# Reordering the first block of a two-block transformer kernel, and sharing the weight split between two engines

## The reference

```python
def first_block(x, c, ...):
    mod = silu(c) @ w_ada + b_ada                 # 2048 -> 6*2048
    shift_m, scale_m, gate_m, shift_f, scale_f, gate_f = split(mod, 6)
    h = rms_norm(x, norm_mix_g) * (1 + scale_m) + shift_m
    q, k, v, xs, z, bmat, cmat, dt_raw = split(h @ w_in)   # 1024 each up to z, 256, 256, 16
    attn = rms_norm(moba_attention(q, k, v, rel_bias), attn_norm_g)    # 8 heads
    ssm = ssd_mixer(xs, z, bmat, cmat, dt_raw, ...)        # 16 heads, conv of 4 taps first
    x = x + gate_m * (concatenate([attn, ssm]) @ w_out)
    h = rms_norm(x, norm_ffn_g) * (1 + scale_f) + shift_f
    x = x + gate_f * conv_ffn(h, w_up, ..., w_down)        # 2048 -> 2*5632 -> 2048
    return rms_norm(x, final_norm_g)

def second_block(x, mem, ...):
    # neighbourhood attention and latent attention side by side, w_out
    x = x + memory_attention(rmsnorm(x), rmsnorm(mem), w_xq, w_xk, w_xv, w_xo)
    x = x + swiglu(rmsnorm(x), w_gate, w_up, w_down)
    return rmsnorm(x, final_norm)
```

## Time and profile before

| | |
|---|---|
| median of 3 runs | 3294.6 us (3288.72 to 3298.83) |
| the profiled execution: span from first to last instruction | 3309.4 us |
| its own time beside the span | no separate time is listed; the span stands for it |
| busy: PE, POOL, ACT, DVE | 88%, 67%, 35%, 34% |
| granted clock of TensorE, mean (1.00 is 2.4 GHz) | 0.930 |

### The profile page before, as it was taken

How to read it: one execution, slowest core, us unless ns; L and a number is a source line. 1 busy time by engine, 2 the same in 40 slices (tenths; PEclk the granted TensorE clock), 3 DMA queues, 4 the chain that set the end, 5 groups by cost and what they waited for, 6 DMA issues and landing times.

```text
span 3309.4 us, 54043 instructions
## 1 busy us (share of the span) xinstructions
PE 2912.6 (88%) x21608; PEld 2795.5 (84%) x21608; DVE 1128.3 (34%) x1286; ACT 1167.9 (35%) x1286; POOL 2220.5 (67%) x889
## 2 busy tenths in 40 slices
PE   4657879896789999999997976698898999999997
PEld 4657769775779999999997975598798999999997
DVE  4688771256855444422213032302102000001222
ACT  2222223332233433334443443233333333333443
POOL 2455768353758889878884843085476888887885
PEclk8778999798999999999998987698999999999999
DMA  7976765432746666545552542053243554554452
GB/s 218 351 267 241 272 250 207 166 142 81 261 176 226 229 219 238 191 164 179 187 180 90 189 129 90 8 221 129 102 164 129 180 187 179 181 187 165 178 184 96
DMA packets 112195, 598.17 MB, mean 181 GB/s; under 512 B 23340, under 2 KB 25388, under 8 KB 54860
## 3 DMA queue, kind: packets, MB, share of 16 engines
q1 hardware_dynamic: 92736, 570.84, 47.4%
q10 hardware_dynamic: 19340, 25.59, 2.7%
HBM read 581.98 MB, written 14.40 MB: 180 GB/s over the span
## 4 chain that ended last, share of the span: by engine, by line
PE 66%; issue 17%; POOL 11%; DVE 5%; ACT 1%; DMA 1%; ACTq 0%; POOLq 0%; DVEq 0%; SPq 0%
PE ps L825 20%; PE ps L827 20%; PE ps L829 20%; POOL w_lo L358 11%; PE ps L884 2%; PE ps L977 1%; PE ps L950 1%; DVE work L1281 1%; PE ps L966 1%; PE ps L841 0%; PE ps L839 0%; PE ps L843 0%; PE ps L954 0%; DVE work L1383 0%; DVE work L1252 0%
## 5 line engine op out<-in xcount | busy, mean ns | idle before, releaser
L358 POOL TENSOR_TENSOR w_lo<-raw,w_hi 128x1024 fp32r<-128x1024 f32 x884 | 2220.1, 2522 | 1054.5 <-ACT w_hi L379 1052.7
L825 PE MATMUL ps<-a_hi,w_hi 128*128 128x256 f32 x6512 | 1882.4, 289 | 236.9 <-DVE a_lo L1273 113.2
L827 PE MATMUL ps<-a_lo,w_hi 128*128 128x256 f32 x6512 | 1871.8, 287 | 0.0
L829 PE MATMUL ps<-a_hi,w_lo 128*128 128x256 f32 x6512 | 1870.7, 287 | 0.5 <-issue 0.5
L825 PEld LDWEIGHTS ps<-a_hi,w_hi 128*128 128x128 f32 x6512 | 1281.2, 197 | 251.6 <-issue 235.7
L379 ACT CAST w_hi<-raw 128x1024 fp32r<-128x1024 f32 x884 | 916.6, 1047 | 1589.8 <-PE ps L829 1080.8
L827 PEld LDWEIGHTS ps<-a_lo,w_hi 128*128 128x128 f32 x6512 | 1281.5, 197 | 0.2
L829 PEld LDWEIGHTS ps<-a_hi,w_lo 128*128 128x128 f32 x6512 | 1280.0, 197 | 0.7 <-issue 0.7
L1216 DVE SCALAR_TENSOR_TENSOR arena<-arena,small 128x1024 f32<-128x1024 f32 x150 | 388.9, 2628 | 105.4 <-DMA arena<-ada 104.5
L1332 DVE TENSOR_TENSOR a_lo<-arena,a_hi 128x1024 fp32r<-128x1024 f32 x44 | 112.7, 2565 | 364.4 <-ACT a_hi L662 364.4
L1652 DVE TENSOR_TENSOR arena<-ps,work 128x512 f32 (+1 forms) x22 | 15.2, 692 | 488.4 <-ACT work L792 488.4
(11 more groups left out here) (126 smaller groups left out, 1183.9 us busy)
## 6 DMA issues: line engine op xcount, KB each, us to landing
raw<-stream SPq DMA_DIRECT2D x442, 1024.0 KB, 4.8
arena<-ada SPq DMA_DIRECT2D x192, 512.0 KB, 4.6
arena<-memT SPq DMA_DIRECT2D x4, 512.0 KB, 7.9
res<-xT SPq DMA_DIRECT2D x1, 2048.0 KB, 20.8
rel_rows<-arena ACTq DMA_DIRECT2D x1, 2048.0 KB
mem_high<-a_hi ACTq DMA_DIRECT2D x1, 2048.0 KB, 46.6
mem_low<-a_lo ACTq DMA_DIRECT2D x1, 2048.0 KB, 24.6
k_spill<-arena ACTq DMA_DIRECT2D x4, 512.0 KB, 5.7
```

What stands on the lines that cost most here:

```text
L358: pool.tensor_tensor(w_lo[:, slot], raw[:, tile_slot, part * HALF:(part + 1) * HALF], w_hi[:, slot].bitcast(F32), ALU.subtract).then_inc(l ...
L825: pe.matmul(o, w_hi[:, slot, w], a_hi[:, c0 + k, :], start=first and k == 0 and f % 2 == 0, stop=False, skip_group_check=True)
L827: pe.matmul(o, w_hi[:, slot, w], a_lo[:, c0 + k, :], start=False, stop=False, skip_group_check=True)
L829: mm = pe.matmul(o, w_lo[:, slot, w], a_hi[:, c0 + k, :], start=False, stop=last and k == 1, skip_group_check=True)
```

## The change

The memory projections `xk` and `xv` both come first and share one normed memory, so nothing is stored to DRAM and fetched back. Then xs, dt, b and c, z; then q, k, v beside the 16 state space heads; then attention beside the half of `w_out` that multiplies the state space output (`wb`); then the other half (`wa`). The two outputs have a norm each (`mixs`, `mixa`), scaled in place. The rows of `w_ada` are spread over the halves by a table (`rows_by`), and their ring of 4 lasts until row 80.

A second part of the same diff touches all stages: the low parts are divided between DVE and POOL by a table per matrix (`LOW_ON_DVE`, period 8 halves), with a semaphore for each (`lo_dve`, `lo_pool`). Matrices that are not in the table stay on POOL. DVE's programs get the call `lows(a, b)` at fixed places. PE no longer waits for `hi_ready` beside the low part. The start of `down` waits for the hidden groups one by one.

```diff
-STREAM = [("xk", 16), ("win", 44), ("dt", 1), ("xv", 16), ("wout", 16), ("up", 88), ("down", 44),
+STREAM = [("xk", 16), ("xv", 16), ("xs", 8), ("dt", 1), ("bz", 12), ("qkv", 24), ("wb", 8), ("wa", 8), ("up", 88), ("down", 44),
...
+LOW_ON_DVE = {"xk": (1, 1, 1, 1, 1, 1, 0, 0), "xv": (1, 1, 1, 1, 1, 1, 0, 0),
+              "xs": (1, 1, 1, 1, 1, 1, 0, 0), "dt": (1,) * 8, "bz": (1, 1, 1, 1, 0, 0, 1, 1),
+              "qkv": (1, 1, 0, 0, 1, 1, 0, 0), "wb": (1, 1, 0, 0, 1, 1, 0, 0),
+              "wa": (1, 1, 0, 0, 1, 1, 0, 0), "up": (0, 0, 1, 1, 0, 0, 1, 1), "down": (0, 0, 1, 1, 0, 0, 1, 1),
+              "gu": (0, 0, 1, 1, 0, 0, 1, 1), "down2": (0, 0, 1, 1, 0, 0, 1, 1)}
...
-ADA_EARLY = 64
+ADA_EARLY = 80
...
+def ssm_until(h):
+    return H0["qkv"] + 6 + 26 * h // 16
+def moba_until(i):
+    if i < 8:
+        return H0["qkv"] + 35 + 13 * (i + 1) // 8
+    return H0["wb"] + 12 * (i - 7) // 8
+ROW_POINTS = [(-1, 0), (2, 0), (3, 10), (7, 16), (55, 64), (67, 64), (75, 70), (83, 75), (91, 82), (105, 96),
+              (108, 96), (112, 100), (140, 128), (143, 128), (168, 152), (176, 158), (181, 160), (186, 160)]
...
 # SP
+                    h, ahead = 2 * t - 2 * RAW + 1, 2 * step
+                    for low, count in ((lo_dve, DVE_COUNT), (lo_pool, POOL_COUNT)):
+                        if count[h] != (count[h - 2] if h > 1 else 0):
...
+                            sp.wait_ge(low, i * more + count[h] if more else count[h])
...
+            def tiles_beside(a, b, issued):
+                for t in range(a, b):
+                    stream_tile(t)
+                    done = rows_by(2 * t - 8)
+                    until = min(160, done + (4 if done + 4 <= ADA_EARLY else 2))
+                    for n in range(issued, until):
+                        ada_row(n)
+                    issued = max(issued, until)
...
 # ACT
-            act.wait_ge(al_ready, 4)
-            act.dma_start(mh_dram, a_hi[:, :, :].bitcast(F32)).then_inc(mem_stored, 16)
-            act.dma_start(ml_dram, a_lo[:, :, :].bitcast(F32)).then_inc(mem_stored, 16)
...
 # DVE
+            def lows(a, b, i=None, step=16):
+                for h in range(a, b):
+                    if ON_DVE[h]:
+                        dve.wait_ge(hi_ready, h + 1 if i is None else i * step + (h + 1))
+                        dve.tensor_tensor(w_lo[:, h % SLOTS], raw_half(h), w_hi[:, h % SLOTS].bitcast(F32),
+                                          ALU.subtract).then_inc(lo_dve, 1)
...
+            def steps(a, b):
+                for h in range(a, b):
+                    lows(h, h + 1)
+                    ada_rows(rows_by(h))
...
             for h in range(STATE_HEADS):
                 mixing(h)
                 if h + 2 < STATE_HEADS:
                     seg(h + 2)
                 if h % 2 == 0 and h:
                     gate_y(h // 2 - 1)
+                steps(ssm_until(h) + 3 if h else hq + 6, ssm_until(h + 1) + 3)
...
+            def up_turn(g0, i=None):
+                for g in range(g0, g0 + 2):
+                    lows(hu + 8 * g + 8, hu + 8 * g + 12 if g < 21 else hu + 8 * g + 10, i)
+                    up_conv(g, i, None if i is None else i * PER_TURN)
+                    if g < 21:
+                        lows(hu + 8 * g + 12, hu + 8 * g + 16, i)
+                    up_gate(g - 1, i)
...
             with dve.Fori(0, 8) as i:
                 last_slice_rows(i)
-                up_turn(i)
+                up_turn(2, i)
```

More of the change, by code:

```diff
@@ L282, in _, with stream_tile, ada_row @@
         def _(sp):
-            def stream_tile(t, slot, first=False):
+            def stream_tile(t, first=False, i=None, step=4):
                 if not first:
[L286 to L295, removed]
+                    h, ahead = 2 * t - 2 * RAW + 1, 2 * step
+                    for low, count in ((lo_dve, DVE_COUNT), (lo_pool, POOL_COUNT)):
+                        if count[h] != (count[h - 2] if h > 1 else 0):
+                            more = 0 if i is None else count[h + ahead] - count[h]
+                            sp.wait_ge(low, i * more + count[h] if more else count[h])
+                sp.dma_start(raw[:, t % RAW], stream[t if i is None else i * step + t])\
+                  .then_inc(raw_landed[t % RAW], 16)
+            def ada_row(n):
+                ring = 4 if n < ADA_EARLY else 2
+                if n >= 4:
+                    sp.wait_ge(ada_used, n + 1 - ring)
+                sp.dma_start(ada_slot(n % ring), ada[n]).then_inc(ada_landed[n % ring], 16)
+            def tiles_beside(a, b, issued):
[6 more added lines that the diff above has]
+                    issued = max(issued, until)
+                return issued
             for q in range(4):
@@ L353, in _, with low_part, low_parts @@
             pool.memset(ones[:, :], 1.0).then_inc(ones_ready, 1)
[L355 to L366, removed]
+            def low_part(h, i=None, step=0):
+                pool.wait_ge(hi_ready, h + 1 if i is None else i * step + (h + 1))
+                pool.tensor_tensor(w_lo[:, h % SLOTS], raw_half(h), w_hi[:, h % SLOTS].bitcast(F32),
+                                   ALU.subtract).then_inc(lo_pool, 1)
+            def low_parts(name, a, b):
+                h0, period = H0[name], 16
+                n = (b - a) // period
+                if n >= 2:
+                    with pool.Fori(0, n) as i:
+                        for h in range(h0 + a, h0 + a + period):
+                            if not ON_DVE[h]:
+                                low_part(h, i, period)
+                    a += n * period
+                for h in range(h0 + a, h0 + b):
+                    if not ON_DVE[h]:
+                        low_part(h)
+            for name, n in STREAM:
+                low_parts(name, 0, 2 * n)
         @block.scalar
@@ L505, in _ @@
[L505 to L521 removed]
+                spill_group(G - 1, k_dram[G - 1] if G <= 4 else v_dram[G - 5])
@@ L1259, in newton, with norm @@
                     settle()
-            def norm(name, source, gain, shift=None, summed=False):
+            def norm(name, source, gain, shift=None, summed=False, between=None):
                 if not summed:
@@ L1438, in _ @@
             norm("mix", lambda c: res[:, c, :], lambda c: mod[:, 0, c:c + 1], lambda c: mod[:, 1, c:c + 1],
-                 summed=True)
-            for g in range(8):
-                if g == 7:
-                    conv_ssm(6, 0, 0)
-                if g == 4:
-                    ada_mod(2)
-                ada_unit(8 + g)
-            conv_ssm(7, 1, 1)
-            ada_mod(3)
-            conv_ssm(10, 2, 0)
+                 summed=True, between=lambda q: lows(hx + 2, hx + 4) if q == 2 else None)
+            steps(hx + 4, hx + 12)
+            conv_ssm("xs", 0, 0, 0)
+            steps(hx + 12, hb + 2)
+            conv_ssm("xs", 1, 1, 1)
+            steps(hb + 2, hb + 4)
             G = G0["dt"]
```

660 lines of the change are left out of this document (380 added, 280 removed).

## The result

The changed kernel is slower: 3395.1 us (3377.2 to 3400.9) against 3292.0 us, a ratio of 1.030, 95% interval 1.027 to 1.033. The forecast was 3215 us and faster, its range ended at 3290. The profiled execution has a span of 3399.1 us.

A forecast was written before the change was run, and what follows sets the result against it. PE was taken to bound `up`, `down` and after; the first block lost 425 us to waits. From a 3309 us span, 138 less there, 60 more in `up` and 2 less gave 3229, times 0.9955: 3215 us, range 3080 to 3290.

The forecast's parts named there:

- a first stretch without gain: Rival: memory projections, bound by transfers, stay at 4.9 us per half; 82 us more, 3296 us, chance 0.07.
- The two places: In `up`, low ahead of convolution and rows after late gate delay PE; turn 46 to 53.5 us, 60 us in all.
- The slack of 0.5 us a group: In `up`, a low 2.4 us late against 1.9 us slack: PE waits 0.5 us per group, without rows left to rounding.
- Rival 4: In `up`, stalls leave PE at 1.2 GHz for one group per turn: 184 us more, 3398 us, chance 0.10.
- The last halves of bz: Last 17 halves of bz: DVE waits for rows issued late behind tiles; 83 us, bounds 57 and 95.
- Beside the heads and in attention: DVE sets the pace, with late rows: 142 us for 26 halves beside heads, 122 for 25 beside attention.
- The term of 5 us per late row: From bz through attention: a late row takes 5 us from issue to use, with the tile issued ahead.
- Attention and `wa`: 25 halves beside attention at DVE's pace, 122 us (bounds 95 and 135); `wa` 47 us.
- The rate of 3.2 us per half: Halves 8 to 55, memory projections: 48 x 3.2 = 154 us, bounds 2.9 and 3.6 per half.
- Start: First 8 halves: 78 us where it was 108, with PE idle for 10 us; bounds 72 and 90.
- PE at 2.88 us a half everywhere: PE's pace at clock 1.00, measured in `up`, used for PE's work in the first block's stages.
- The rule against the change: DVE and POOL share a read port, so moved lows save nothing; as a rival 3269 us, chance 0.08.

The follow-up runs named there:

- 5: Changed kernel with every low part on POOL and SP issuing the needed row ahead of the tile: 3221.8 us, ratio 0.979 to the kernel before.
- experiment 4: Changed kernel with the `w_ada` rows in `up` issued and used two by two, behind each convolution: 3340.2 us, ratio 1.011 to the kernel before.
- 9: On top of experiment 4, DVE's lows in `up` cut to the last pair of each group: 3304.4 us, ratio 1.002 to the kernel before.
- experiment 3: Changed kernel with SP issuing the needed row ahead of the next tile: 3312.0 us, ratio 1.005 to the kernel before.
- 8: Changed kernel with rows 96 to 159 of `w_ada` loaded and accumulated in 16 of 1024 columns, part of the computation left out: 3327.3 us.
- 11: Changed kernel with rows 16 to 63 of `w_ada` loaded and accumulated in 16 of 1024 columns, part of the computation left out: 3376.8 us.
- 2: Changed kernel with every low part on POOL: 3260.0 us, ratio 0.988 to the kernel before.
- 6: Changed kernel with low parts shared in all but `up` and the needed row issued ahead of the tile: 3222.5 us, ratio 0.979 to the kernel before.
- 1: Changed kernel with all low parts of `up` on POOL: 3303.4 us, ratio 1.001 to the kernel before.
- 7: On top of 5, SP issues tiles 4 and 5 ahead of the residual input and rows 4 and on: 3207.9 us, ratio 0.974 to the kernel before.
- 10: On top of 7, the fourth vector of the modulation made ahead of the output norm's Newton steps: 3213.3 us, ratio 0.975 to the kernel before.
- 12: On top of 10, the first `w_ada` rows spread later (4 by half 3, 8 by half 7): 3222.1 us, ratio 0.979 to the kernel before.

## Why the prediction was wrong

The direction was wrong because a gain of 138 us in the first block was 4 us (7 us at half 186, where `up` starts), while the loss in `up` was 98 us for 60. No rival said this; the nearest, a first stretch without gain, ended at 3296. The 134 us by which the first block missed are spread: 14 at the start, 26 in halves 8 to 56, 12 to half 89, 16 at the heads, 29 in attention, 6 and 20 in `wb` and `wa`, 13 at norm `ffn`, and 2 the other way. Two faults can be taken out, the lows on DVE (40 us, half 190 at 917) and the rows behind the tiles (74 us, at 883); without both it comes at 876 us (5), still 53 later than forecast.

- **`up`: the mechanism was right, the size of the turn off.** A turn was forecast at 53.5 us and took 56.6 to 59.5. The two places were named, the rows between gate and lows (experiment 4: 55 us of the 92) and the low ahead of the convolution (the 36 us that 9 gave back, with the reserve told there). The stalls, 3.1 and 3.2 us, add up to 6.3 where 7.5 were forecast for the turn. What was mis-sized is what follows a stall: the granted clock in these turns is 0.93, the first matmul after each stall has 0.58 us for 0.28. Some 4 us a turn are left for that when the stalls are taken from the difference of 11. The prediction had this as a rival and put it at nothing in its own sum. The slack of 0.5 us a group was set down as nothing in the turns without rows; one took 47.6 us. Rival 4's mechanism, a clock that falls after each stall, is present at a sixth of its price.
- **The last halves of bz: right.** 83 forecast, 81 measured. The late row was found from the order of SP's queue: DVE waits 40 us for rows between 400 and 475 us, and experiment 3 takes the stretch to 66.
- **Beside the heads and in attention: right cause, too small.** The term of 5 us per late row was 6.05 in the row shown, since row and tile land later there: the median from issue to landing is 5.8 us between 474 and 850 us, against 3.8 in the earlier trace rows. Row order alone gave back 67 us of 445 (experiment 3). In the forecast late rows were in the sum already, so these 67 us don't explain a miss; they show that without this fault the block would have gained 78 us, somewhat over half of what I had claimed with it.
- **Attention and `wa`: the step that failed most, 29 and 20 us.** I priced each stage as the sum of its busiest engine. With rows in time (3) or thin (8) the stretch of attention from 141 to 166 still takes 129 to 130 us, where my lower bound for it was 95. There PE waits for DVE's softmax, scaling and low parts one after the other, which no sum over one engine contains. In `wa` the wait for the low parts of the scaled output, 7.7 us, was laid beside three halves and taken as hidden. The term of 47 is PE's own pace for 16 halves (46 us) and has no row. By the high parts of the kernel before, its last 16 halves of `w_out` took 62 us, and from there to half 190, with norm `ffn`, 35 where 25 stands in the sum: 97 together, 72 forecast, 105 measured. So 25 of the 33 us missed there were a gain for which the sum gives no reason.
- **The first stretch: 26 us off.** The rate of 3.2 us per half was to come from 28 us per 8 halves at 302 GB/s, taken down to 25.6. It moved 305 GB/s. I went below the row without a row for it; at 3.5 us it would have been 168 of the 180. But that the rate came out equal doesn't make 302 GB/s the limit: 373 GB/s stand in the next line, and with thin rows (11), at 211 GB/s, the stretch is only 18 us shorter. All lows on POOL (2) make it 11 us shorter. The rest of its pace is open.
- **Start: 14 us off.** PE idle for 26.5 us, not 10. Ten rows with their landings were put at some 15 us, and the wait for row 4 alone was 16.0 us. The 108 us of before were laid to ACT's queue alone, and that was a part of it: SP held tile 4, which half 8 needs, behind twelve rows, and when ACT was free at 90.9 us the high part had to wait for that tile. Timeline of SP, then of ACT, in the kernel before:

```profile
54.64 35.82 SPq L295 DMA_DIRECT2D arena<-ada  x12
90.83 0.35 SPq L287 DMA_DIRECT2D raw<-stream  x1
...
107.78 1.99 ACT L379 CAST w_hi<-raw 128x1024 fp32r<-128x1024 f32 x2 [8.16 <-DMA raw<-stream]
```

- **PE at 2.88 us a half everywhere.** Between 294 and 919 us the granted clock is 0.84 to 0.90. Before, too, it was low in the stages with gaps (0.73 to 0.94), and those stages should have been priced by that.
- **The rule against the change** was given 0.08 as a cause of a smaller gain. By 5 and 6 its result, no gain from the sharing, came out over the whole, but not its mechanism: halves 8 to 56 went at 3.7 us, not 3.9, and at 3.5 without the sharing. While rows were late the sharing did worse than nothing: 92 us in `up` and 43 in the first block.

Open is why halves 8 to 56 take 3.4 us each with thin rows, and what of the 43 us between 1 and 2 is meetings and what is order.

## What to carry to other kernels

A job that is moved to an engine with in-order work doesn't cost its duration, it costs its place: ask what stands ahead of it, when that can start, and what is queued behind. Where one queue issues transfers for two consumers, a wait for one of them holds the other's data; issue first what is needed first. An engine that also issues stores can be held by the issue itself, here 31 us, so look at its issuing queue before a stall is laid to the data. A stage without a saturated engine can't be priced by its busiest engine; walk one period of it through all queues, as was done for `up`, where it came out nearly right.

## What the runs showed of the hardware

**An issue that holds its engine.** Two stores of bias rows are issued by ACT at the start, `rel_rows` and `rpb_rows`, the second in packets of 508 bytes, which go out from 42 to 107 us in the changed kernel, and from 45 to 122 us in 7. The next issue on ACT's queue takes 31.5 us when it is made at 58.9 us (before), 31.1 to 32.3 us at 73.5 to 75.1 us (7, 10, 12), but 1.8 us at 99.6 us (changed) and 3.0 us at 98.7 us (5). All this fits an issue that waits until the small packets are nearly out; that the store is the cause was not tried.

**Slow rows at the start.** The rows of `w_ada` land slowly there although little is asked for: between 45 and 92 us the DMA engines are busy 0.79 at 205 GB/s, between 272 and 294 us 0.93 at 373 GB/s. In the fastest kernel (7), in the 65 us from 45 on, rows take 8.1 us to land and tiles 10.0. The answer on transfers of that kernel, by queue and by issue:

```profile
DMA packets 6864, 15.03 MB, mean 231 GB/s; under 512 B 3682, under 2 KB 3682, under 8 KB 6458
...
q1 hardware_dynamic: 2805, 11.90, 50.8%
q10 hardware_dynamic: 4056, 3.10, 32.3%
...
arena<-ada SPq DMA_DIRECT2D x18, 512.0 KB, 8.1
raw<-stream SPq DMA_DIRECT2D x4, 1024.0 KB, 10.0
```

ACT's queue (q10) takes 32.3% of the engines' time for 3.1 MB, SP's (q1) 50.8% for 11.9 MB. By the trace's packets, q10 has 3364 of 508 bytes (`rpb_rows`, 1.7 MB, 10.5%) and 678 of 2048 bytes (`rel_rows`, 1.4 MB, 21.7%, the last at 79 us), so the smallest packets are not the larger part of it. That these stores are what holds the first rows was not tried.
